# The second conditioning product on GpSimd instead of VectorE

## The reference

```
# first block: one conditioning row, 6 vectors in each of 2 layers
cond = silu(c);  mod = cond @ ada_w[i] + ada_b[i]
x = x + g1 * mixer(rms_norm(x) * (1 + sc1) + sh1)      # conv, then attention
x = x + g2 * (square(relu(h @ mlp_w1[i])) @ mlp_w2[i])
# second block: two conditioning rows, 3 vectors in each of 2 layers
cond = silu(c_2);  cond_ctx = silu(c_ctx_2)
mod  = cond @ ada_w_2[i] + ada_b_2[i];  mod_c = cond_ctx @ ada_w_2[i] + ada_b_2[i]
```

## Time and profile before

| | |
|---|---|
| median of 3 runs | 1210.99 us (1209.44 to 1213.26) |
| the profiled execution, its own time | 1210.95 us |
| its span, first to last instruction | 1209.1 us |
| TensorE busy | 1182.7 us, 98% of the span |
| VectorE busy | 910.7 us, 75% |
| ScalarE busy | 592.4 us, 49% |
| GpSimd busy | 63.2 us, 5% |
| mean granted clock of TensorE | 0.990 of full speed |

### The profile page before, as it was taken

One profiled execution on the slowest core, in us unless ns is written; L12 is line 12 of the kernel. 1 busy time (PEld: TensorE's weight loads), 2 busy tenths in 40 slices (PEclk: granted clock), 3 DMA queues, 4 the chain that ended last, 5 costly groups with the idle time before them and its releaser, 6 DMA issues.

```text
span 1209.1 us, 18282 instructions
## 1 busy us (share of the span) xinstructions
PE 1182.7 (98%) x7490; PEld 1015.2 (84%) x7490; DVE 910.7 (75%) x1371; ACT 592.4 (49%) x792; POOL 63.2 (5%) x93
## 2 busy tenths in 40 slices
PE   8998999999999999999999999999999999999997
PEld 6976988888988869889999888888888888898776
DVE  6879688888878676899987674876757675677767
ACT  4566666556544375765465422332212323454773
POOL 0211000000000040000000000000000000000640
PEclk9999999999999999999999999999999999999998
DMA  9896467787768604666775454333453342332000
GB/s 372 294 356 238 175 264 284 284 326 261 279 227 316 216 26 175 244 244 248 263 255 175 144 204 139 139 111 134 140 174 140 105 142 102 131 140 105 2 1 36
DMA packets 34726, 230.06 MB, mean 190 GB/s; under 512 B 4161, under 2 KB 4929, under 8 KB 8402
## 3 DMA queue, kind: packets, MB, share of 16 engines
q1 hardware_dynamic: 33874, 227.14, 52.1%
q0 software_dynamic: 768, 1.75, 0.5%
HBM read 226.08 MB, written 1.05 MB: 188 GB/s over the span
## 4 chain that ended last, share of the span: by engine, by line
PE 82%; DVE 8%; DMA 4%; ACT 3%; issue 2%; POOL 1%; SPq 0%; ACTq 0%; DVEq 0%
PE prod L1866 16%; PE prod L1860 15%; PE prod L1862 15%; PE prod L1861 15%; PE prod L1867 8%; DMA raw<-stream 4%; DVE w_lo L1061 2%; PE prod L1877 1%; PE misc L2022 1%; ACT w_hi L624 1%; PE misc L2124 1%; PE misc L1775 1%; PE prod L2112 1%; PE misc L1819 1%; PE prod L2099 1%
## 5 line engine op out<-in xcount | busy, mean ns | idle before, releaser
L1061 DVE TENSOR_TENSOR w_lo<-raw,w_hi 128x2048 fp32r<-128x2048 f32 x131 | 300.1, 2290 | 204.0 <-ACT w_hi L624 203.6
L624 ACT ACTIVATE w_hi<-raw 128x2048 fp32r<-128x2048 f32 x131 | 250.9, 1915 | 397.6 <-PE prod L1862 230.3
L1860 PE MATMUL prod<-X_both,w_hi 128*128 128x256 f32 (+1 forms) x656 | 218.0, 332 | 3.8 <-DVE w_lo L1061 2.1
L1861 PE MATMUL prod<-X_both,w_hi 128*128 128x256 f32 (+1 forms) x656 | 214.5, 327 | 0.0
L1862 PE MATMUL prod<-X_both,w_lo 128*128 128x256 f32 (+1 forms) x656 | 214.4, 327 | 0.0
L1866 PE MATMUL prod<-X_both,w_hi 128*128 128x512 f32 x592 | 211.4, 401 | 1.2 <-DVE X_both L1294 0.7
L1867 PE MATMUL prod<-X_both,w_lo 128*128 128x256 f32 x592 | 166.2, 281 | 0.0
L1860 PEld LDWEIGHTS prod<-X_both,w_hi 128*128 128x128 f32 x656 | 124.5, 190 | 18.8 <-DVE w_lo L1061 3.7
L1866 PEld LDWEIGHTS prod<-X_both,w_hi 128*128 128x128 f32 x592 | 111.5, 188 | 30.2 <-DVE X_both L1294 1.1
L1861 PEld LDWEIGHTS prod<-X_both,w_hi 128*128 128x128 f32 x656 | 124.6, 190 | 10.9 <-issue 0.5
L1862 PEld LDWEIGHTS prod<-X_both,w_lo 128*128 128x128 f32 x656 | 124.5, 190 | 10.7
(11 more groups left out here) (336 smaller groups left out, 1992.0 us busy)
## 6 DMA issues: line engine op xcount, KB each, us to landing
raw<-stream SPq DMA_DIRECT2D x202, 1024.0 KB, 4.9
V<-first_chunks SPq DMA_DIRECT2D x8, 512.0 KB, 12.1
X<-x_features SPq DMA_DIRECT2D x1, 1024.0 KB, 5.1
raw<-first_chunks SPq DMA_DIRECT2D x2, 512.0 KB, 6.3
C<-first_chunks SPq DMA_DIRECT2D x2, 512.0 KB, 17.1
V<-cond_rows SPq DMA_DIRECT2D x1, 1024.0 KB
C<-ctx_features SPq DMA_DIRECT2D x1, 1024.0 KB, 7.0
out_features<-HT SPq DMA_DIRECT2D x4, 256.0 KB, 2.2
```

The lines of the kernel that those rows point to most:

```text
L624: A(halves(w)[0], raw[:, n % RING, :].rearrange("p (k c) -> p k c", k=KT), ACT.Copy).then_inc(weight_hi, 1)
L1061: ins = tt(lo, raw[:, n % RING, :].rearrange("p (k c) -> p k c", k=KT), hi.bitcast(F32), ALU.subtract)
L1860: mm(out, lhs_hi, rhs_hi, start=start, stop=False)
L1861: mm(out, lhs_hi, rhs_lo, start=False, stop=False)
```

## The change

The product of the second conditioning rows and their sigmoid is taken from VectorE's step 65 and given to GpSimd, in GpSimd's list between the first and the last attention. GpSimd waits until `mod_step` says that the last vector of the first block is summed (which VectorE does ahead of unit 64), and for the sigmoid. VectorE waits for the finished product in `dots`, ahead of every half of a chunk of the second kind.

```diff
@@ gpsimd
             for p in range(KT):
                 ...
                     scale(m, m, sm[:, p % 3, 10 + t:11 + t], None, ALU.mult).then_inc(alibi_scaled_pool, 1)
+            pool.wait_ge(mod_step, MOD_DONE[BLOCK_2 - 1])
+            pool.wait_ge(cond_sigmoid, 2)
+            nc.gpsimd.tensor_tensor(cond[:, :, :], cond_t, cond_2, ALU.mult).then_inc(cond_ready, 1)
             pool.wait_ge(acts_lo, SET[10])
@@ vector
-            def silu_cond(part, dst, c, t):
-
-                dve.wait_ge(cond_sigmoid, part)
-                tt(dst, t, c, ALU.mult).then_inc(cond_ready, 1)
-                dve.wait_ge(cond_ready, part)
-
@@ dots
                     if block_no == 2:
+                        dve.wait_ge(cond_ready, 2)
                         vec.tensor_tensor_reduce(scrap, w, cond[:, 0, :], 1.0, 0.0, ALU.mult, ALU.add,
@@ steps of VectorE
-                if s == COND_2_UNIT - 1:
-                    dve.wait_ge(mod_step, MOD_DONE[BLOCK_2 - 1])
-                    silu_cond(2, cond[:, :, :], cond_2, cond_t)
```

## The result

| | before | after |
|---|---|---|
| median of 20 runs | 1209.68 us (1206.94 to 1214.02) | 1213.89 us (1211.68 to 1216.41) |
| ratio | | 1.0029, 95% interval 1.002 to 1.0038 |
| span of the profiled execution | 1209.1 us | 1209.9 us |

By the ratio the changed kernel is slower by 0.29%, 3.5 us, with an interval from 2.4 to 4.6 us (the medians alone lie 4.2 us apart). The two profiled spans differ by only 0.8 us. They can't be compared whole: the profiled execution of after happened to reach the change 3.3 us earlier (its subtraction of unit 64 starts at 498.43, that of before at 501.77). So I read the stretch around the change, and count from a common event.

A forecast was written before the change was run, and what follows sets the result against it. The prediction took TensorE, busy 98% of the span, as the bound. Removing the VectorE product (-0.7 us) and delaying unit 64's subtraction (+2.1) gave +1.4 us on 1210.95: 1212.4 us, range 1209.4 to 1215.2.

The forecast's parts named there:

- The sign of the balance: Around units 64 to 66, the removal's gain of 0.7 us was outweighed by 2.1 us of delay: slower by 1.4 us.
- the likeliest case: At unit 64's subtraction, VectorE at half pace beside GpSimd: delay 1.2 to 2.2 us, net +0.5 to +1.5, chance 0.35.
- no difference: Whole kernel: a change within 0.3%, or 3.6 us, given chance 0.86, against faster 0.02 and slower 0.12.
- rival 2: At unit 64, VectorE held for GpSimd's reads or whole length: net +2.3 to +3.4, +4.0 to +5.1 with fallen clock; chance 0.27.
- So GpSimd can hold VectorE up, but not through its whole operation: Read from the last attention: L1613 took 0.82 instead of 0.42 us, ending 0.6 us before the GpSimd operation did.
- the term of +2.1 us: Unit 64's subtraction on VectorE, at half pace while GpSimd runs, ends at 506.1 instead of 504.06, adding to TensorE's wait.
- The product's own time: The moved product on GpSimd from 500.5 to 505.9, 5.4 us, continued from rows of operations with one input.
- No slack stands between that subtraction and TensorE: VectorE's subtraction of unit 64 ends at 504.06, TensorE starts at 504.12: any delay passes on one for one.
- The clock: After a long TensorE stand at unit 64, some 3.4 us at 1.2 GHz, matmuls at half pace, costing 1.7 us.
- Minus 0.7 us: Removing VectorE's 2.29 us product makes TensorE's 0.70 us wait for unit 66 vanish, with 1.4 us to spare.
- Nothing was swallowed later: Behind unit 66 TensorE is busy almost without waits up to 900 us, so a shift at 516 reaches the end whole.
- The 48 waits ahead of the dots: VectorE's added waits before the dot products, 1.4 to 4.8 us spread over 470 us, covered by gained room, costed at nothing.

The follow-up runs named there:

- the pieces: The changed kernel with the GpSimd product split into 8 instructions of 256 columns; ratio to before 0.999, 1208.78 against 1209.53 us.
- later_start: The changed kernel, but GpSimd also waits until VectorE has finished the low half of unit 64; ratio to before 1.0007, 1210.94 against 1210.48 us.
- extra_product: The kernel before, its product still on VectorE, plus the same product on GpSimd, thrown away; ratio to before 1.002, 1212.29 against 1209.53 us.
- the filled one: The changed kernel with 8 overwritten matmuls on TensorE ahead of its wait for unit 64; ratio to before 1.0015, 1210.27 against 1209.53 us.
- ScalarE's version: No GpSimd product; ScalarE writes Silu of the two rows into cond in its step 65; ratio to before 0.9975, 1207.03 against 1209.53 us.

## Why the prediction was right or wrong

**The sign of the balance and the range: right; the likeliest case: wrong.** The time lies in the range, and 0.29% lies inside "no difference", but by a hair: the interval, 0.20 to 0.38%, reaches past the 0.3% that the forecast had drawn. There is luck in the range too. The forecast counted from 1210.95, and before came out at 1209.68 over 20 runs; 1210.95 and the 4.47 of the ruler would be 1215.4, above the range. And the forecast's case (VectorE at half pace, +1.4 us) didn't happen; rival 2, held for the whole length with the fallen clock, did.

**"So GpSimd can hold VectorE up, but not through its whole operation" is the step that failed**, and with it the term of +2.1 us. The row was read rightly, and carried over wrongly: L1613 stood behind an instruction with one tensor in, the product has two. (L1583, which "took its usual 0.48", scales one tensor itself, so it was no row for a subtraction of two.) The runs show held to the end for two (2.15 and 2.16 us of VectorE's work left at GpSimd's end), let in 1.7 us early for one. The ratio 0.82 over 0.42 taken from it was no pace but a short stand seen against a short operation; the pieces show that no pace is shared. The price was 3.17 us (5.46 less 2.29) and not 2.1.

The Trainium skill (SBUF — State Buffer, Summary: rules for kernel authors) says of a VectorE instruction with two SBUF inputs and a GpSimd one that reads SBUF that the second to issue is fully blocked until the first finishes. The traces agree for two tensors (delay 3.17 us) and don't for one (let in 1.7 us before the end). The limit that the Trainium skill sets to this (SBUF — State Buffer, Who interferes with whom), that a GpSimd instruction which only writes doesn't contend, agrees as well (2.29 us beside 5.55 us of memsets).

Which of two comes first can't be told from the starts alone. L1349 in `later_start` started 0.34 us behind GpSimd's product and was held. L1613 at 1136.76 also started 0.34 behind GpSimd's scaling and took its usual 0.42, while the scaling took 2.13 instead of 1.88. Why the second got ahead no run here shows.

**The product's own time.** 5.4 us predicted, 4.60 measured. Rival 2's whole hold was 4.1 us with 5.4; with 4.60 it is 3.3 (498.43 to GpSimd's end at 501.74), where 3.17 was measured. My continuation of the scaling rows was right for one tensor of 2048 columns (5.37 and 5.46 us), and not for two. The Trainium skill's 4497 ns for an add of this size (GPSIMD Engine Reference, 3.1 Elementwise) was nearer.

**"No slack stands between that subtraction and TensorE"**: right, and decisive. The stand grew by 3.37 us for 3.17 of delay.

**The clock**: right as rival 2 had it, 1.7 us predicted, 2.2 measured in unit 64 (7.94 less 5.76) and 1.5 in `extra_product`. That it follows from the stand is shown by the filled one; why it cost more in one execution than in the other isn't.

**"Minus 0.7 us. This part I hold for safe."** The wait did vanish (0.96 in the ruler, of which 0.70 are the wait), but the removal wasn't needed for it: it vanishes just so with the product left on VectorE. The gain and the loss were not two terms to be added. Once the loss has made TensorE late, there is no wait left to gain. Where the loss is avoided (pieces), the product comes late and the wait stays; only ScalarE's version collects it.

**The sum** of the ruler: +3.36 (stand) + 2.18 (clock) - 0.96 - 0.11 = +4.47, against the -0.7 + 2.1 of the forecast. Nothing was swallowed later, as said. The 48 waits ahead of the dots cost nothing that shows: the dot product behind the small operations starts 0.60 us after the start of the one ahead of it in after (507.82 to 508.42) and 0.59 in before (516.86 to 517.45), where no such wait stands.

## What to carry to other kernels

Before work goes to GpSimd because it is idle, list what VectorE does in that time with both inputs in SBUF, and which of it has slack: here 4.6 us on an idle engine cost 3.2 on a subtraction that had none. When a row shows one engine delaying another, note how many tensors each instruction reads before carrying it over. And look for an operation that does the whole thing on an engine that already passes over the data: one ScalarE function replaced two operations and was faster than both kernels.

## What the runs showed of the hardware that I had not expected

- A two-tensor product on GpSimd (4.60 us) kept a two-input VectorE instruction out until its end: 5.46, 5.45, 5.42 and 4.95 us instead of 2.29, and 4.82 instead of 0.68. A scaling of one tensor (5.46 us) let it in after 3.7 us. Three memsets (5.55 us) didn't delay it.
- A GpSimd scaling of 2048 columns of one tensor (5.37 and 5.46 us) takes longer than a product of two (4.60 to 4.75).
- Eight pieces of 256 columns took 10.73 us beside a busy VectorE for the work of 4.60: VectorE gets in at each seam, GpSimd waits.
- A stand of TensorE of 3.8 us brought 6.8 us at the lower clock in one execution (from 2.0 us into the stand, unit 64 in 7.94 us) and 3.4 in another of the same length (from 1.1 us behind its end, unit 64 in 7.28 us). One of 1.6 us brought none.
